# Expert passes of 112 tokens in place of 128 in a two-layer decoder trunk on one Trainium2 core

## The reference

```python
logits = (t @ w_router).astype(jnp.float32)
top_val, top_idx = lax.top_k(logits, TOP_K)            # TOP_K = 2 of N_EXPERTS = 8
top_w = jax.nn.softmax(top_val, axis=-1)
for e in range(N_EXPERTS):                              # combine: top_w scattered to (256, 8)
    out = out + combine[:, e:e + 1] * _swiglu(t, wg[e], wu[e], wd[e])
```

## Time and profile before

| | before |
|---|---|
| median of 3 runs | 1432.94 us (1431.57 to 1433.2) |
| span of the profiled execution | 1432.2 us |
| TensorE busy, matmul | 1401.6 us (98%) |
| TensorE busy, loads of stationary blocks | 1137.3 us (79%) |
| VectorE busy | 1232.6 us (86%) |
| ScalarE busy | 900.5 us (63%) |
| GpSimd busy | 45.5 us (3%) |
| DMA moved | 484.50 MB, mean 338 GB/s |
| mean granted TensorE clock | 0.998 |

### The profile page before, as it was taken

One profiled execution on the slowest core, in us unless ns is written; L12 is line 12 of the kernel. 1 busy time (PEld: TensorE's weight loads), 2 busy tenths in 40 slices (PEclk: granted clock), 3 DMA queues, 4 the chain that ended last, 5 costly groups with the idle time before them and its releaser, 6 DMA issues.

```text
span 1432.2 us, 18313 instructions
## 1 busy us (share of the span) xinstructions
PE 1401.6 (98%) x6882; PEld 1137.3 (79%) x6882; DVE 1232.6 (86%) x1087; ACT 900.5 (63%) x794; POOL 45.5 (3%) x79
## 2 busy tenths in 40 slices
PE   5989999999999999999999999999999999999999
PEld 2774899996775888888888888888888888888886
DVE  3679677776888898999999999999999999999997
ACT  3073534343274677777777777777777777777774
POOL 0000000000000000000000000000000000000012
PEclk9999999999999999999999999999999999999999
DMA  9976669779628899999999999999999999999995
GB/s 367 401 303 211 246 224 372 266 263 364 241 77 295 291 366 375 358 393 395 341 395 396 340 397 394 391 347 393 393 342 396 396 340 397 394 381 357 394 392 149
DMA packets 195824, 484.50 MB, mean 338 GB/s; under 512 B 8926, under 2 KB 31684, under 8 KB 191684
## 3 DMA queue, kind: packets, MB, share of 16 engines
q1 hardware_dynamic: 187056, 451.17, 84.2%
q0 software_dynamic: 6480, 32.52, 6.1%
q10 hardware_dynamic: 2244, 0.22, 0.1%
HBM read 473.40 MB, written 10.49 MB: 338 GB/s over the span
## 4 chain that ended last, share of the span: by engine, by line
PE 91%; DVE 4%; DMA 3%; ACT 1%; issue 1%; SPq 0%; DVEq 0%; ACTq 0%
PE ps L1052 21%; PE ps L1054 21%; PE ps L1053 21%; PE ps L865 4%; PE ps L709 4%; DMA arena<-in_w_ada 3%; PE ps L903 2%; PE ps L902 2%; PE ps L904 2%; PE ps L1095 2%; PE ps L702 2%; PE ps L910 1%; PE ps L912 1%; PE ps L911 1%; DVE split_r L1810 1%
## 5 line engine op out<-in xcount | busy, mean ns | idle before, releaser
L1970 DVE TENSOR_TENSOR split_r<-arena,split_r 128x2048 fp32r<-128x2048 f32 x336 | 763.5, 2289 | 61.9 <-ACT split_r L1380 61.4
L1380 ACT ACTIVATE split_r<-arena 128x2048 fp32r<-128x2048 f32 x334 | 640.4, 1918 | 125.1 <-PE ps L1054 121.9
L1052 PE MATMUL ps<-split_r,tokens_r 128*128 128x512 f32 x1280 | 505.4, 395 | 0.0
L1054 PE MATMUL ps<-split_r,tokens_r 128*128 128x512 f32 x1280 | 499.2, 390 | 0.0
L1053 PE MATMUL ps<-split_r,tokens_r 128*128 128x512 f32 x1280 | 498.2, 389 | 0.0
L1054 PEld LDWEIGHTS ps<-split_r,tokens_r 128*128 128x128 f32 x1280 | 240.2, 188 | 51.1
L1053 PEld LDWEIGHTS ps<-split_r,tokens_r 128*128 128x128 f32 x1280 | 240.6, 188 | 47.8
L1052 PEld LDWEIGHTS ps<-split_r,tokens_r 128*128 128x128 f32 x1280 | 240.5, 188 | 47.9 <-DVE split_r L1970 0.4
L902 PE MATMUL ps<-tokens_r,split_r 128*128 128x256 f32 x352 | 99.2, 282 | 0.2 <-DVE split_r L1810 0.2
L903 PE MATMUL ps<-hT_r,split_r 128*128 128x256 f32 x352 | 99.3, 282 | 0.0
L904 PE MATMUL ps<-tokens_r,split_r 128*128 128x256 f32 x352 | 98.6, 280 | 0.0
(11 more groups left out here) (359 smaller groups left out, 1317.6 us busy)
## 6 DMA issues: line engine op xcount, KB each, us to landing
arena<-in_moe_w_gate SPq DMA_DIRECT2D x57, 2048.0 KB, 10.6
arena<-in_moe_w_up SPq DMA_DIRECT2D x57, 2048.0 KB, 10.7
arena<-in_moe_w_down SPq DMA_DIRECT2D x56, 2048.0 KB, 10.3
arena<-in_w_ada POOLq DMA_DIRECT2D x10, 1536.0 KB, 10.0
arena<-in_w_ada SPq DMA_DIRECT2D x14, 1024.0 KB, 17.0
arena<-in_ffn_w_gate SPq DMA_DIRECT2D x11, 1024.0 KB, 6.1
arena<-in_ffn_w_up SPq DMA_DIRECT2D x11, 1024.0 KB, 13.1
arena<-in_ffn_w_down SPq DMA_DIRECT2D x11, 1024.0 KB, 14.3
```

Of the source, the lines that this page charges most:

```text
L1052: mm(out_, xh, h, start=first, stop=False, skip_group_check=True)
L1054: return mm(out_, xl, h, start=False, stop=last_, skip_group_check=True)
L1380: A(wh[:, j % SPLITS, :], piece_half(j), ACT.Copy).then_inc(sem("w_hi"), 1)
L1970: v.tensor_tensor(wl[:, j % SPLITS, :], piece_half(j), wh[:, j % SPLITS, :].bitcast(F32), ALU.subtract).then_inc(sem("w_lo"), 1)
```

## The change

A constant `CAP = 112` takes the place of 128 as the number of tokens in a pass. The stationary blocks of the expert matmuls have 112 columns; outputs, hidden values and `ynat` stand on 112 partitions; the transposed tiles `hTh`, `hTl` and `fTs` are packed at 112 columns a block, and the transposes use a 112 x 112 corner of the identity. The 512 moving columns of weights and the 128 rows of the contraction stay. Since 2 x 112 is under 256, an expert may have up to three passes; the routing adds a comparison (`third`) and one addition, and `iota` has to reach 336, its further values standing in columns that `colA` used earlier.

```diff
+CAP = 112
+    assert SEQ <= 3 * CAP < SEQ + 126
-        iota = sb("iota", SEQ + 1)
-        colA = sb("colA", 126)
+        iota = sb("iota", SEQ + 1 + 126)
+        colA = iota[:, SEQ + 1:]
-        y_rows = nc.dram_tensor("y_rows", (2 * NE, P, D), F32, kind="Internal").ap()
+        y_rows = nc.dram_tensor("y_rows", (2 * NE, CAP, D), F32, kind="Internal").ap()
-        hTh = part(tokensr, 0, KD, P)
-        hTl = part(tokensr, KD * P, KD, P)
-        fTs = part(tokensr, 2 * KD * P, 2, EFT * P)
+        hTh = part(tokensr, 0, KD, CAP)
+        hTl = part(tokensr, KD * P, KD, CAP)
+        fTs = part(tokensr, 2 * KD * P, 2, EFT * CAP)
-        e_tg = part(F, 2048, EW)
-        e_hid = part(F, 2560, EW)
+        e_tg = part(F, 2048, EW)[0:CAP, :]
+        e_hid = part(F, 2560, EW)[0:CAP, :]
...
             # GpSimd
+            g.iota(iota[:, SEQ + 1:3 * CAP + 1], pattern=[[1, 3 * CAP - SEQ]], base=SEQ + 1, ...)
-            pool.wait_ge(sem("no_outputs"), 2)
+            pool.wait_ge(sem("no_outputs"), 3)
-                g.indirect_dma_start(hrow, None, h_rows, bass.IndirectOffsetOnAxis(ap=slot_row[:, 0:1], axis=0))\
+                g.indirect_dma_start(hrow, None, h_rows, bass.IndirectOffsetOnAxis(ap=slot_row[0:CAP, 0:1], axis=0))\
...
             # TensorE
-                    last = tr(ps[:, 2 + k // 4, (k % 4) * P:(k % 4 + 1) * P], hrow[:, k * P:(k + 1) * P], ident[:, :])
+                    last = tr(ps[:, 2 + k // 4, (k % 4) * CAP:(k % 4 + 1) * CAP], hrow[:, k * P:(k + 1) * P],
+                              ident[0:CAP, 0:CAP])
-                                last = triple(ps[:, 4 + n, :], *(x_[:, ff * P:(ff + 1) * P] for x_ in fT_parts(c)),
+                                last = triple(ps[0:CAP, 4 + n, :], *(x_[:, ff * CAP:(ff + 1) * CAP] for x_ in fT_parts(c)),
-                            last = triple(ps[:, 2 * (c % 2) + (kind == "u"), :], hTh[:, kk, :], hTl[:, kk, :],
+                            last = triple(ps[0:CAP, 2 * (c % 2) + (kind == "u"), :], hTh[:, kk, :], hTl[:, kk, :],
-                            last = tr(ps[:, 6 + c % 2, f * P:(f + 1) * P], e_hid[:, f * P:(f + 1) * P], ident[:, :])
+                            last = tr(ps[:, 6 + c % 2, f * CAP:(f + 1) * CAP], e_hid[:, f * P:(f + 1) * P],
+                                      ident[0:CAP, 0:CAP])
...
             # ScalarE
-                        A(fT_parts(turn_after[j])[0], ps[:, 6 + turn_after[j] % 2, :], ACT.Copy)\
+                        A(fT_parts(turn_after[j])[0], ps[:, 6 + turn_after[j] % 2, 0:EFT * CAP], ACT.Copy)\
...
             # VectorE, routing
-                v.tensor_scalar(per, ps[:, 2, 2 * NE:3 * NE], float(P), 1.0, ALU.is_gt, ALU.add)
+                v.tensor_scalar(per, ps[:, 2, 2 * NE:3 * NE], float(CAP), 1.0, ALU.is_gt, ALU.add)
+                third = part(F, 2708, NE)
+                v.tensor_scalar(third, ps[:, 2, 2 * NE:3 * NE], float(2 * CAP), None, ALU.is_gt)
                 ...
+                link(v.tensor_tensor(per, per, third, ALU.add))
-                link(v.tensor_scalar(first_of, first_of, 1.0, None, ALU.min))
+                link(v.tensor_scalar(first_of, first_of, 2.0, None, ALU.min))
                 ...
+                dve.wait_ge(sem("no_outputs"), 3)
-                slots = iota[:, bass.ds(second * P + 1, P)]
+                slots = iota[:, bass.ds(second * CAP + 1, CAP)]
-                        v.tensor_tensor(low_, ps[:, 6 + c % 2, :], high.bitcast(F32), ALU.subtract)\
+                        v.tensor_tensor(low_, ps[:, 6 + c % 2, 0:EFT * CAP], high.bitcast(F32), ALU.subtract)\
```

More of the change, by code:

```diff
@@ L204, in trunk @@
         fl = part(Fr, 2 * FT * SEQ, 2, FT * SEQ)
-        hTh = part(tokensr, 0, KD, P)
-        hTl = part(tokensr, KD * P, KD, P)
-        fTs = part(tokensr, 2 * KD * P, 2, EFT * P)
+        hTh = part(tokensr, 0, KD, CAP)
+        hTl = part(tokensr, KD * P, KD, CAP)
+        fTs = part(tokensr, 2 * KD * P, 2, EFT * CAP)
         hnat = part(F, 0, NT, D)
-        e_tg = part(F, 2048, EW)
-        e_hid = part(F, 2560, EW)
[L212 to L215, removed]
+        e_tg = part(F, 2048, EW)[0:CAP, :]
+        e_hid = part(F, 2560, EW)[0:CAP, :]
+        fTs_last = part(Fr, 2048, 2, EFT * CAP)
+        sel = part(F, 3072, NT, P)[:, :, 0:CAP]
+        swT = part(F, 3328, NT * P)[0:CAP, :]
+        blank = part(tokens, 2 * D, D)[0:CAP, :]
         w_row = rs[:, 32:36].rearrange("p (t c) -> p t c", t=NT)
-        slot_now = rs[:, 36:38]
-        slot_next = rs[:, 38:40]
-        hrow = part(F, 0, D)
+        slot_now = rs[0:CAP, 36:38]
+        slot_next = rs[0:CAP, 38:40]
+        hrow = part(F, 0, D)[0:CAP, :]
         rowbuf = part(work, 12800, 512)
@@ L528, in _ @@
                             pattern=[[-1, P]], channel_multiplier=1).then_inc(sem("consts"), 1)
-            g.iota(iota[:, :], pattern=[[1, SEQ + 1]], base=0, channel_multiplier=0,
+            g.iota(iota[:, 0:SEQ + 1], pattern=[[1, SEQ + 1]], base=0, channel_multiplier=0,
                    allow_small_or_imprecise_dtypes=True).then_inc(sem("consts"), 1)
@@ L1017, in gather @@
                     for t in range(NT):
-                        last = mm(ps[:, 2 + k // 4, (k % 4) * P:(k % 4 + 1) * P], hnat[:, t, k * P:(k + 1) * P],
+                        last = mm(ps[:, 2 + k // 4, (k % 4) * CAP:(k % 4 + 1) * CAP], hnat[:, t, k * P:(k + 1) * P],
                                   sel[:, t, :], start=(t == 0), stop=(t == NT - 1))
@@ L1026, in slot_rows @@
                 for t in range(NT):
-                    last = mm(ps[:, 7, 0:2], sel[:, t, :], w_row[:, t, :], start=(t == 0), stop=(t == NT - 1))
+                    last = mm(ps[0:CAP, 7, 0:2], sel[:, t, :], w_row[:, t, :], start=(t == 0), stop=(t == NT - 1))
                 last.then_inc(sem("row_ps"), 1)
@@ L1385, in high_h @@
                     act.wait_ge(sem("gath_ps"), 2 * p + half + 1)
-                    A(hTh[:, half * 4:half * 4 + 4, :].rearrange("p k n -> p (k n)"), ps[:, 2 + half, :], ACT.Copy)\
+                    A(hTh[:, half * 4:half * 4 + 4, :].rearrange("p k n -> p (k n)"), ps[:, 2 + half, 0:4 * CAP], ACT.Copy)\
                         .then_inc(sem("hT_hi"), 1)
@@ L1947, in experts @@
                                      ALU.add))
-                link(v.tensor_scalar(most, inc[:, NE - 1:NE], float(P), -float(P), ALU.mult, ALU.add))
+                link(v.tensor_scalar(most, inc[:, NE - 1:NE], float(CAP), -float(CAP), ALU.mult, ALU.add))
                 link(v.tensor_scalar(kept, slot, most, None, ALU.is_le))
-                link(v.scalar_tensor_tensor(out=slot, in0=slot, scalar=float(P - 1), in1=kept, op0=ALU.add, op1=ALU.mult))
+                link(v.scalar_tensor_tensor(out=slot, in0=slot, scalar=float(CAP - 1), in1=kept, op0=ALU.add, op1=ALU.mult))
                 v.tensor_copy(out_row[:, :], slot.rearrange("p t r -> p (t r)")).then_inc(sem("out_row"), 1)
@@ L1975, in low_half @@
                 dve.wait_ge(sem("hT_hi"), 2 * p + half + 1)
-                v.tensor_tensor(hTl[:, half * 4:half * 4 + 4, :].rearrange("p k n -> p (k n)"), ps[:, 2 + half, :],
+                v.tensor_tensor(hTl[:, half * 4:half * 4 + 4, :].rearrange("p k n -> p (k n)"), ps[:, 2 + half, 0:4 * CAP],
                                 hTh[:, half * 4:half * 4 + 4, :].rearrange("p k n -> p (k n)").bitcast(F32),
@@ L1997, in weigh @@
                 cols = slice(512 * n, 512 * n + 512)
[L1998 removed]
+                return v.scalar_tensor_tensor(out=ynat[:, cols], in0=ps[0:CAP, 4 + n, :], scalar=slot_now[:, 0:1],
                                               in1=gate_row[:, cols], op0=ALU.mult, op1=ALU.mult)
@@ L2019, in one_pass @@
                         b = 2 * (c % 2)
-                        v.scalar_tensor_tensor(out=e_tg, in0=e_tg, scalar=1.0, in1=ps[:, b, :], op0=ALU.add,
+                        v.scalar_tensor_tensor(out=e_tg, in0=e_tg, scalar=1.0, in1=ps[0:CAP, b, :], op0=ALU.add,
                                                op1=ALU.mult).then_inc(sem("e_mid"), 1)
                         dve.wait_ge(sem("e_mid"), p * ECHUNKS + c + 1)
-                        v.scalar_tensor_tensor(out=e_hid, in0=e_tg, scalar=0.5, in1=ps[:, b + 1, :], op0=ALU.mult,
+                        v.scalar_tensor_tensor(out=e_hid, in0=e_tg, scalar=0.5, in1=ps[0:CAP, b + 1, :], op0=ALU.mult,
                                                op1=ALU.mult).then_inc(sem("e_hid"), 1)
@@ L2039, in one_pass @@
                         dve.wait_ge(sem("slot_now"), p + 1)
-                        v.tensor_scalar(swT, iota[:, 0:SEQ], slot_now[:, 1:2], None, ALU.is_equal)
+                        v.tensor_scalar(swT, iota[0:CAP, 0:SEQ], slot_now[:, 1:2], None, ALU.is_equal)
                     if not final or j + SPLITS < HP:
```

25 lines of the change are left out of this document (13 added, 12 removed).

## The result

The changed kernel takes 1447.55 us (median of 4 runs, 1445.62 to 1447.69) against 1432.31 us before (4 runs): the ratio is 1.0104, 95% interval 1.0093 to 1.0116. It is slower by 15 us where 10.8 us less were forecast. The number lies beside the rival "odd blocks, slower" (1444 us), which had been given 0.16.

The account below looks back on a forecast made before the run. TensorE's own pace was taken to bound the expert stage; -6.0 (matmuls) - 3.7 (transposes) - 0.9 (restarts) - 0.5 (slot rows) + 0.3 (added work) = -10.8 us from 1432.94 gave 1422.1 us, range 1411 to 1438.

Parts of the forecast that it names:

- odd blocks, slower: Rival: loads from blocks packed every 448 bytes never settle, expert matmul spacing about 4 ns up, 1444 us; chance 0.16.
- What bounds the kernel: Expert stage: only TensorE's instruction-to-instruction time sets the 118.99 us pass period; no TensorE wait within a pass.
- The 4032 matmuls: Expert matmuls over 8 passes: loading 112 instead of 128 columns takes 1.5 ns off each, 6.0 us less.
- the unsettled starts behind each restart: Matmuls right behind a group of transposes start 0.23 us apart before settling at 0.227; kept, 16 us more.
- Transposes, restarts, slot rows: 280 transposes moving 112 columns, 3.7 us less; shorter first loads behind transposes or slot rows, 0.9; L1027's 2-column matmuls, 0.5.
- Added work: Routing ahead of the loop: one comparison and one linked addition on VectorE, 0.3 us more, between 0 and 0.5.
- the stop at 484.64: Ahead of the loop, TensorE waits once for VectorE's split: L1052 starts at 484.64 where 484.48 was due.
- Copies, rows, DMA: ScalarE and VectorE copies, POOL's stored and gathered rows, and DMA run beside the matmuls or off the chain: 0.
- Number of passes: Largest expert has 106 tokens, under 112, so 8 passes and no cost; a ninth would cost 119 us.

Follow-up runs that it names:

- w1_wide_blocks: Changed kernel with 128-column loaded blocks back on their old places and copies 512 wide, transposes still moving 112 columns; 1429.09 us, 0.9975 of before.
- p1_packed_full: Changed kernel, buffers on old places, blocks packed every 448 bytes, 128-column loads (112 for each tile's last block), first half piece waiting for both token halves; 1445.98 us.
- a3_aligned_stride: Changed kernel with `split` and `tokens` on their old places and 112-column blocks starting every 512 bytes; 1434.89 us, 1.0017 of before.
- a1_aligned: Changed kernel with the spacer made 64 bytes, so `split` and `tokens` are on their old places, blocks still packed; 1444.46 us, 1.0087 of before.
- b_load112: Kernel before, with only the `triple` matmuls loading and putting out the first 112 columns of each block; 1440.42 us.

## Why the prediction was wrong, step by step

- **What bounds the kernel** was right: TensorE's spacing sets the pass, to 10 ns, before and after. No wait came to TensorE in a pass.
- **The 4032 matmuls** is the step that failed, in sign. It read the 13.5 ns above the streaming time as the load taking turns, costing by the column, and took off 1.5 ns. Measured: +4.35 ns each, +2.15 us a pass, 17 us in all where -6.0 was put. Loads of 64 columns, 54 ns shorter in themselves, at a spacing of 230 ns refute the reading. The rows under it compared two lengths and two formats, none of which varied the columns loaded.
- **The Trainium skill's rule** on this ("TensorE: Matmul & The Clock Gate", section "What happens when you issue a matmul": the next block's load takes no bandwidth from the running matmul) agrees with the runs only in that fewer columns gain nothing. It would have kept the spacing at 0.227 us, though, and fewer columns bring 229.6 to 233.3 ns, a load 32 bytes elsewhere 233: load and stream are not independent in this kernel. Where page and run differ, the run decides.
- **Odd blocks**, the rival at 1444 us, had the right place and nearly the right price: +4 ns forecast, +4.35 measured. The price was in part luck: it was lent from the distances behind a restart, and its cause, the packing, was only part of it. The packing costs 1.9 us a pass at full length (w1_wide_blocks to p1_packed_full) or 1.27 at 112 columns (a3_aligned_stride to a1_aligned); the shorter load by itself costs 0.84 us (w1_wide_blocks to a3_aligned_stride) or 1.11 (before to b_load112). It got 0.16 although the unsettled starts behind each restart spoke for it: I used them for its price alone, and not to doubt that 0.227 is a sum of costs of which a part can be taken off.
- **Transposes, restarts, slot rows** were forecast at 5.1 us in all. The transposes' spacing came out at 0.096 us as said, but the matmul behind a group starts 0.03 us after its last transpose with either length, so 28 count a pass, not 36. Measured: transposes and slot rows 0.40 us a pass, restarts 0.11, together 4.1 us.
- **Added work** of 0.3 us: the stop at 484.64 is gone in the changed kernel, where that matmul starts at 484.48; nothing can be told of the link, below what these runs tell apart.
- **Copies, rows, DMA** at 0: right. ScalarE and VectorE sank by 0.6 and 0.4 us a pass, and TensorE waits for neither in a pass.
- **Not foreseen at all**: the joined `iota` and `colA` moved all later tensors by 32 bytes, 1.7 us in the dense stage. The diff shows the joining; I had taken it as free.
- **Number of passes**: eight, as taken.

## What to carry to other kernels

In a stream of full-rate fp32r matmuls that each load a block, treat the steady spacing as a rhythm between the load and the moving side: keep loaded blocks 128 columns wide and at the distance from the moving operand at which it is even (here a multiple of 512 bytes), even when fewer columns are needed, and shorten only what is paid by the column, such as transposes. When tensors are added or joined, compare the start addresses of all later ones: 32 bytes moved a stage that nobody had edited. And before a cost per matmul is scaled with a size, find or make a run that varies that size alone.

## What the runs showed of the hardware that was not expected

- With all else equal, moving the loaded operand by 32, 64 or 128 bytes against the moving one took the spacing of 128x512 fp32r matmuls from 227.3 to 233 ns (period 118.99 to 121.7 to 121.9 us); moving both by 32 bytes left it at 227.2 on the blocks that moved along, and 24 matmuls of a pass on blocks that stayed behind went to 233.3. With 112-column loads, moving both by 32 bytes made 230.2 of 229.2.
- The spacing with 120, 112, 96 and 64 loaded columns was 233.3, 229.6, 230.0 and 230.1 ns: none below that of 128.
- The spacing of fp32 transposes went with their moving columns: 0.109 us at 128 and 0.096 us at 112, with 128 loaded columns in both; with 96 loaded columns it was 0.109 us at 128 moving ones too.
